# Longer weight runs, byte masks, later zero stores and separate column tiles in a diffusion backbone with recurrence and experts

## What is computed

```
sh1, sc1, g1, sh2, sc2, g2 = split(silu(cond) @ w_mod[l] + b_mod[l])
h  = rms_norm(x, norm1) * (1 + sc1) + sh1
... = split(h @ w_in[l])          # attention q, k, v; recurrence q, f, f', i, g; two gates
x += g1 * ((sig(ga) * (attn @ w_br_attn) + sig(gh) * (rec @ w_br_hgrn)) @ w_out[l])
h  = rms_norm(x, norm2) * (1 + sc2) + sh2
gates = top-1 group, then top-2 of its 4 experts, from sigmoid(h @ w_router)
x += g2 * sum_e gates[e] * (silu(h @ w_gate[e]) * (h @ w_up[e])) @ w_down[e]     # 16 experts, D_FF 512
```

## Time and profile before

| what | value |
|---|---|
| median of 3 runs | 1604.6 us (1602.77 to 1606.4) |
| the profiled execution's own time | 1598.92 us |
| its span | 1597.1 us |
| TensorE busy | 1401.8 us, 88% of the span |
| VectorE busy | 519.8 us |
| ScalarE busy | 335.0 us |
| GpSimd busy | 240.2 us |
| moved by DMA | 351.96 MB, mean 220 GB/s |

### The profile page before, as it was taken

The page is one execution under the profiler, slowest core; times in us unless marked ns, Lnnn a source line. Parts: engine busy times, 40 slices in busy tenths (PEclk is TensorE's granted clock), DMA queues, the critical chain, the costliest instruction groups (busy, mean ns, idle before and its releaser), DMA issues.

```text
span 1597.1 us, 18517 instructions
## 1 busy us (share of the span) xinstructions
PE 1401.8 (88%) x7179; PEld 768.5 (48%) x7180; DVE 519.8 (33%) x1041; ACT 335.0 (21%) x495; POOL 240.2 (15%) x213
## 2 busy tenths in 40 slices
PE   4699999899998899989965999988999598999882
PEld 1365545656554444544423655566654344444441
DVE  1333423744113411121125344278311521111114
ACT  1105533651101100100101065265100100001010
POOL 2260003841000000000012600186100000000001
PEclk9899999999999899999986999999999899999996
DMA  9635453176424999996984331211414444999994
GB/s 344 246 109 189 181 208 109 53 253 261 158 106 150 363 380 396 399 339 248 398 304 156 109 106 54 106 53 53 145 53 158 184 166 177 339 396 397 396 395 178
DMA packets 157043, 351.96 MB, mean 220 GB/s; under 512 B 5880, under 2 KB 13128, under 8 KB 156992
## 3 DMA queue, kind: packets, MB, share of 16 engines
q1 hardware_dynamic: 138208, 314.48, 53.0%
q0 software_dynamic: 6576, 22.80, 4.0%
q10 hardware_dynamic: 12208, 13.98, 2.6%
HBM read 335.69 MB, written 15.55 MB: 220 GB/s over the span
## 4 chain that ended last, share of the span: by engine, by line
PE 71%; DVE 10%; SPq 7%; DMA 6%; ACT 3%; issue 2%; POOL 0%; DVEq 0%; ACTq 0%; POOLq 0%
PE pG L1401 21%; PE pS L1481 10%; PE pG L1393 9%; SPq L472 6%; PE pG L1496 5%; PE pG L1623 5%; PE pG L1489 4%; DMA ring<-in_w_mod_dram 2%; PE pX L1322 2%; PE pX L1481 2%; DVE ring L1005 2%; PE pG L1355 2%; DMA ring<-in_w_exp_up_dram 1%; DVE modb L1007 1%; PE pX L1447 1%
## 5 line engine op out<-in xcount | busy, mean ns | idle before, releaser
L1401 PE MATMUL pG<-hT,ring 128*128 128x384 f32 x896 | 299.5, 488 | 1.6 <-ACT gen L842 1.6
L1481 PE MATMUL pS<-ring,gen 128*64 128x256 f32 x2048 | 229.8, 381 | 11.5 <-DMA ring<-in_w_exp_up_dram 9.5
L1401 PEld LDWEIGHTS pG<-hT,ring 128*128 128x128 f32 x896 | 168.0, 191 | 115.5 <-issue 4.7
L1481 PEld LDWEIGHTS pS<-ring,gen 128*64 128x64 f32 x2048 | 148.1, 138 | 100.5 <-issue 19.2
L1393 PE MATMUL pG<-ring,hT 128*128 128x512 f32 (+1 forms) x384 | 150.0, 548 | 1.4 <-DVE hT L964 0.7
L1496 PE MATMUL pG<-ring,gen 128*64 128x512 f32 x512 | 116.9, 598 | 5.2 <-DVE gen L1278 5.2
L1273 DVE TENSOR_TENSOR gen<-pS,gen 128x256 f32<-128x256 f32 x32 | 13.6, 425 | 313.4 <-PE pS L1481 313.4
L1393 PEld LDWEIGHTS pG<-ring,hT 128*128 128x128 f32 x384 | 72.6, 192 | 72.1 <-issue 67.7
L660 POOL DMA_INDIRECT gen<-y_scr,idx x12 | 11.8, 985 | 628.5 <-ACTq L892 625.5
L1489 PE MATMUL pG<-hrow,gen 128*64 128x512 f32 x408 | 95.4, 603 | 2.2 <-DVE gen L1173 1.5
L871 ACT COPY gen<-pG 128x512 f32<-128x512 f32 x32 | 18.8, 586 | 348.6 <-PE pG L1496 348.6
(11 more groups left out here) (276 smaller groups left out, 1655.8 us busy)
## 6 DMA issues: line engine op xcount, KB each, us to landing
ring<-in_w_exp_up_dram SPq DMA_DIRECT2D x32, 2048.0 KB, 20.4
ring<-in_w_exp_down_dram SPq DMA_DIRECT2D x32, 2048.0 KB, 19.2
ring<-in_w_exp_gate_dram SPq DMA_DIRECT2D x32, 2048.0 KB, 18.3
ring<-in_w_mod_dram SPq DMA_DIRECT2D x24, 2048.0 KB, 9.4
ring<-in_w_in_dram SPq DMA_DIRECT2D x20, 2048.0 KB, 8.4
modb<-mod_scr POOLq DMA_DIRECT2D x20, 512.0 KB, 9.2
y_scr<-gen ACTq DMA_DIRECT2D x72, 128.0 KB, 5.5
ring<-in_w_out_dram SPq DMA_DIRECT2D x4, 2048.0 KB, 10.1
```

Of the source, the lines that this page charges most:

```text
L1401: ins = pe.matmul(ps[:, 0:TOK], w[:, k, c0:c0 + P], src[:, k, :], start=(k == 0), stop=(k == nk - 1))
L1481: ins = pe.matmul(dst[64 * hf:64 * hf + 64, 0:256], x[:, k, :], w[:, k, 256 * hf:256 * (hf + 1)], start=(k == 0), stop=(k == KC - 1))
```

## The change

- Expert gate and up weights are loaded with rows 8p to 8p+7 in partition p, one run of 16 KB; down weights as two runs of 8 KB. The order of the 1024 features and of the 512 hidden values changes to match: the second norm writes `hrow` in permuted order, with a stride of 512 bytes from one element to the next, and the product of gate and up writes with the same stride between the two values of a pair. The router weights are loaded in the matching order, one run of 512 bytes in each partition.
- The masks come as bytes and straight into `masks`, without the int32 detour through `ring` and without the cast.
- The zero stores to `y_scr` move from the head of ACT's program to SP, behind the load of the `ff` weights.
- On POOL the norm weight now waits for the first `w_mod` piece and so does x, and the small tensors wait for the fourth.
- The four bias products of a `mod` go to four column tiles; the two sums of a pair go to column tiles 0 and 1.

```
-                    src = a[("w_exp_gate", "w_exp_up")[part]][L, e, :, :].rearrange("(k p) n -> p k n", p=P)
-                    dst = ring[:, s0 + part, :].rearrange("p (k n) -> p k n", k=KC)
+                    src = a[("w_exp_gate", "w_exp_up")[part]][L, e, :, :].rearrange("(p k) n -> p (k n)", p=P)
+                    dst = ring[:, s0 + part, :]
                 else:
-                    src = a["w_exp_down"][L, e, :, :].rearrange("(k p) n -> p k n", p=P)
-                    dst = ring[:, s0 + part, :].rearrange("p (k n) -> p k n", k=4)
+                    src = a["w_exp_down"][L, e, :, :].rearrange("(a p c) n -> p a (c n)", a=2, p=P)
+                    dst = ring[:, s0 + part, :].rearrange("p (a m) -> p a m", a=2)
...
                     unit(L, name)
+                    if (L, name) == (0, ("ff", 0)):
+                        sp.wait_ge(zeroed, 1)
+                        for i, r in enumerate(range(NE * BLK, YROWS, P)):
+                            sp.dma_start(y_scr[r:r + P, :].rearrange("p (a c) -> p a c", a=4),
+                                         bc(zeros, [P, 4, 256], 1)).then_inc((*e_ydma, v_dma)[i % 3], 16)
...
+            pool.wait_ge(landed[0], 16)
             load_norm(0, 0)
-            pool.wait_ge(landed[1], 16)
             pool.dma_start(xs[:, 0, :], a["x_prompt"][0]).then_inc(x_in, 16)
             pool.dma_start(xs[:, 1:3, :], a["x_sample"][0].rearrange("(t p) c -> p t c", p=P)).then_inc(x_in, 16)
+            pool.wait_ge(landed[3], 16)
...
-            pool.dma_start(wr[:, :, :], a["w_router"].rearrange("(k p) e -> p k e", p=P)).then_inc(small_in, 16)
+            pool.dma_start(wr[:, :, :], a["w_router"].rearrange("(p k) e -> p k e", p=P)).then_inc(small_in, 16)
...
-            pool.dma_start(masks32, a["masks"]).then_inc(small_in, 16)
+            pool.dma_start(masks[:, :, :].rearrange("p s t -> p (s t)"), a["masks"]).then_inc(small_in, 16)
...
-                act.copy(mod_parts(m)[0:32, :], ps[0:32, :]).then_inc(ms_evac, 1)
+                r = 32 * (m % 2)
+                act.copy(mod_parts(m)[r:r + 32, :], ps[r:r + 32, :]).then_inc(ms_evac, 1)
...
-                    link(dve.scalar_tensor_tensor(hrow[:, t, :], xs[:, t, :], stat[:, t:t + 1], modb[:, 1, cnd, :],
-                                                  ALU.mult, ALU.mult))
-                    dve.tensor_tensor(hrow[:, t, :], hrow[:, t, :], modb[:, 0, cnd, :], ALU.add).then_inc(h_ready, 1)
+                    if which == 0:
+                        h, x, scale, shift = hrow[:, t, :], xs[:, t, :], modb[:, 1, cnd, :], modb[:, 0, cnd, :]
+                    else:
+                        h = hrow[:, t, :].rearrange("p (k c) -> p c k", k=KC)
+                        x, scale, shift = (v.rearrange("p (c k) -> p c k", k=KC)
+                                           for v in (xs[:, t, :], modb[:, 1, cnd, :], modb[:, 0, cnd, :]))
+                    link(dve.scalar_tensor_tensor(h, x, stat[:, t:t + 1], scale, ALU.mult, ALU.mult))
+                    dve.tensor_tensor(h, h, shift, ALU.add).then_inc(h_ready, 1)
...
-                    dve.tensor_copy(masks[:, :, :].rearrange("p s t -> p (s t)"), masks32).then_inc(masks_ready, 1)
-                    dve.wait_ge(masks_ready, 1)
...
-                        dve.tensor_tensor(actb, bank[3][:, 0:256], gsil, ALU.mult).then_inc(e_act, 1)
+                        dve.tensor_tensor(by_pairs(actb), pairs(bank[3][:, 0:256]), pairs(gsil),
+                                          ALU.mult).then_inc(e_act, 1)
...
-                                  w[:, 2 * q + k, :], start=(k == 0), stop=(k == 1 and q > 0))
-                for j in range(4):
-                    r = 4 * (m % MODS) + j
-                    ins = pe.matmul(ps[0:32, P * j:P * (j + 1)], ident[:, r:r + 1].broadcast_to([P, 32]),
-                                    brow[:, m // MODS, :], start=False, stop=(j == 3))
+                                  w[:, 2 * q + k, :], start=(k == 0), stop=False)
+                for q in range(4):
+                    r = 4 * (m % MODS) + q
+                    ins = pe.matmul(ps[32 * q:32 * q + 32, P * q:P * (q + 1)], ident[:, r:r + 1].broadcast_to([P, 32]),
+                                    brow[:, m // MODS, :], start=False, stop=True)
...
-                finish_group(pe.matmul(ps[0:32, :], const[:, C_SEL:C_SEL + 32], mod_parts(m),
+                r = 32 * (m % 2)
+                finish_group(pe.matmul(ps[r:r + 32, :], const[:, C_SEL:C_SEL + 32], mod_parts(m),
                                        start=True, stop=True))
```

More of the change, by code:

```diff
@@ L142, in shape_constants @@
         c[:, C_SIN + HD * t:C_SIN + HD * (t + 1)] = np.sin(ang[t * P:(t + 1) * P]) * sign
-    masks = np.zeros((P, LEV_STEPS, P), np.int32)
+    masks = np.zeros((P, LEV_STEPS, P), np.uint8)
     s, t = np.arange(P)[:, None], np.arange(P)[None, :]
@@ L259, in build @@
         zeros = S[:, 7936:8192]
-        masks32 = S[:, 0:LEV_STEPS * P].bitcast(I32)
         pG = [ctx.enter_context(nc.psum_tensor(f"pG{i}", [P, 512], F32)) for i in range(2)]
@@ L273, in build @@
         cst_ready = sem("cst_ready")
-        masks_ready = sem("masks_ready")
         lb_ready = sem("lb_ready")
@@ L674, in _ @@
             act.sem_inc(e_y, 1)
-            act.wait_ge(zeroed, 1)
-            for i, r in enumerate(range(NE * BLK, YROWS, P)):
-                act.dma_start(y_scr[r:r + P, :].rearrange("p (a c) -> p a c", a=4),
-                              bc(zeros, [P, 4, 256], 1)).then_inc((*e_ydma, v_dma)[i % 3], 16)
             act.wait_ge(setup_in, 16 * 5)
@@ L703, in mod_store @@
                     dst = mod_scr[m // MODS, cnd:cnd + 1, 512 * (m % MODS):512 * (m % MODS + 1)]
-                    act.dma_start(dst, mod_parts(m)[16 * cnd:16 * cnd + 1, :]).then_inc(mod_stored[m % 2], 16)
+                    act.dma_start(dst, mod_parts(m)[r + 16 * cnd:r + 16 * cnd + 1, :]).then_inc(mod_stored[m % 2], 16)
             def mods_behind(L, kind):
@@ L1181, in xT_src, with pairs, by_pairs @@
                     return bank[b].rearrange("p (c a s) -> p c a s", c=4, a=2)
+                def pairs(x):
+                    return x.rearrange("p (q c) -> p q c", c=2)
+                def by_pairs(x):
+                    return x.rearrange("p (c q) -> p q c", c=2)
                 def aT_dst(dst):
@@ L1296, in _ @@
                                 dve.wait_ge(v_act, b + 1)
-                                dve.tensor_tensor(act_o, bank[7][:, 0:256], gsil_o, ALU.mult).then_inc(v_dve, 1)
+                                dve.tensor_tensor(by_pairs(act_o), pairs(bank[7][:, 0:256]), pairs(gsil_o),
+                                                  ALU.mult).then_inc(v_dve, 1)
                                 dve.wait_ge(v_pe, b * 5 + 7)
```

## The result

The changed kernel takes **1580.8 us** (median; 1578.8 to 1582.4) where the kernel before, run beside it, takes 1605.5 (1602.8 to 1606.6). The ratio is 0.9848, with an interval of 0.9831 to 0.9866: 24.7 us faster. The forecast was 1573 with a range of 1564 to 1590, so the number is inside the range. It lies just above the 1568 to 1580 that the forecast called its own, and nearer to the price of rival 1 (1587) than to 1573.

The account below looks back on a forecast made before the run. TensorE was taken to bound the kernel (71% of the wait chain), with DMA at the start and in layer 1's last experts. 13.5 + 5.1 + 1.2 + 0.6 + 11.1 = 31.5 us off 1604.6 gave 1573, range 1564 to 1590.

Parts of the forecast that it names:

- rival 1: Second norm and overflow blocks: the stride costs a second cycle per element, 1.07 us for each of 12 instructions; 1587, chance 27%.
- Start, 13.5 and 0.6 for piece 3: Kernel start: clearing loads ahead of the fourth modulation piece saves 13.5 us; spreading piece 3's bias saves 0.6.
- Column tiles, 5.1: Modulation pieces 4 to 11: bias spread over four column tiles saves 0.64 us per piece, 5.1 us in all.
- Experts of layer 1, 11.1: Last experts of layer 1: long weight runs load fast enough that TensorE never waits, 11.1 us off.
- the experts loaded ahead: Expert weights, layer 1: two experts loaded ahead are worth 12.6 us of slack before the first wait.
- The fitted price per packet (10 ns): DMA queues: 10 ns per packet and 0.0386 ns per byte, giving 15.3 us per expert, or 428 GB/s.
- Rivals 2 and 4: Expert loads: (2) long runs no faster, period 16.55, 1584, chance 9%; (4) 16 KB runs slower than 2 KB, 1625, 4%.
- rival 3: Kernel start: it shortens little, small tensors land late or the fourth piece keeps its time; 1587, chance 9%.
- It pays nothing for the stride, and I take 0.: Second norm, both layers: writes and reads with 512 bytes between elements cost 0, judged from a 12-element memset.
- the rivals' bound of 1 us: Strided product of gate and up in four overflow blocks, not covered by TensorE's gather: 0 to 1 us.

Follow-up runs that it names:

- ScalarE's version: Changed kernel with contiguous second norm and natural router weights; ScalarE writes a reordered copy of the rows behind the router for the gathers: 1569.5 us, ratio 0.9773.
- before, again: The kernel before, unchanged, in a second profiled execution: 1607.6 us.
- start alone: Kernel before with only the first stage's loads and masks changed; column tiles, expert loads and second norm as before: 1589.7 us, ratio 0.9896.
- start and tiles: Kernel before with the changed start and the column tiles for bias and sums; expert loads and norm as before: 1580.8 us, ratio 0.9840.
- long runs, no stride: Kernel before with changed start, column tiles and long expert weight runs, without strided writes; output not the reference's, one block less: 1550.5 us, ratio 0.9665.
- strided reads: Changed kernel with second norm and gate times up writing contiguously and reading in steps (32 B, 8 B) instead: 1582.3 us, ratio 0.9847.
- strided, zero stores first: Changed kernel with the zero stores of y_scr (3.1 MB) back at the head of ScalarE's queue: 1586.6 us in one execution.
- strided, small tensors early: Changed kernel with small tensors and masks no longer held until the fourth modulation piece has landed: 1579.6 us in one execution.
- copy strided: Changed kernel with the reordering moved from the second norm to the copy of the gathered rows, weights in 8 KB runs: 1581.4 us, ratio 0.9853.
- the same, operation done twice: Kernel with the reordering in the copy of gathered rows, plus the second norm's first operation done twice, contiguous: 1592.8 us, ratio 0.9926.
- six patterns: Changed kernel with the second norm in six access patterns, one per tile; output not the reference's, total not compared.
- TensorE's stride: Changed kernel with contiguous second norm; TensorE's router transposes and gathers read the rows in steps of 32 B: 1678.2 us in one execution.

## Why the prediction was right, and where it failed

- **Start, 13.5 and 0.6 for piece 3.** Right, if rather low: 14 to 16 us in the traces against the first profile (2.6 more against the second), 16.9 in the medians. The fourth piece came at 32.7 (forecast 33), the first projection at 51.3 (52). The small tensors were issued from 32.7 us, and VectorE waited for nothing at 50. How the 13.5 divides is less sure: the working had some 10 for the zero stores, and put back alone they cost 6.7; with the 1 to 3 of the small tensors that leaves 5 us or more that no run takes apart. TensorE's first projections ran longer in after, 33.4 us for 31.2 by the chain, with a granted clock of 0.75 in their first 9 us. That is not the change's: six of the eleven executions with the new start took 31.0, and the second one of the kernel before took 33.1.
- **Column tiles, 5.1.** Right: a pair of pieces with its sums takes 5.8 us for 7.1 (107.82 to 113.64, and 120.95 to 128.04 before), 0.64 a piece as worked out, and the stretch with the eight pieces was 5.5 us shorter.
- **Experts of layer 1, 11.1.** Right in mechanism: 426 GB/s for a forecast 428, TensorE never waits, all periods 14.75. The trace of after has 12.4 us against one profile of before and 10.9 against the other, ScalarE's version 10.8 to 11.2. The queue still takes longer for an expert than TensorE (6.55 MB at 426 GB/s are 15.4 us); the experts loaded ahead cover it, as worked out. The fitted price per packet (10 ns) held. By the rule in the Trainium skill (DMA: Bandwidth & Descriptors, "Why small descriptors are slow (HBM only)") the estimate was 413 GB/s; the measurement decides, and a packet costs more than that rule says. Rivals 2 and 4 are out, and rival 3 by the start.
- **"It pays nothing for the stride, and I take 0."** This step failed. Four memsets of 12 elements were taken as the measure of 1024 elements, and they don't show it: at the norm's 0.66 ns for each element they would have taken 8 ns more than they did. Whether they are too short or a memset is another case isn't shown. Twelve instructions pay 0.68 us, 8.2 in all. Rival 1 had the mechanism right but a price of 1.07, more than half as much again. The overflow blocks pay as the rivals' bound of 1 us said: the strided product takes 0.60 us for 0.43 in each of four, 0.7 in all.
- **What the sum left out even so.** From the change to ScalarE's version it is 12 us by the ratios, uncertain by some 5, where 8.2 are VectorE's own. The traces say more. Behind the norm stands a router whose products run at the clock that TensorE was left with. Its sixteen products and the first expert's sixty-four in layer 1, in the kernel before and then in after:

```profile
1261.27 5.32 PE L1631 MATMUL pS<-hT,wr 128*16 128x384 f32 x16 [0.77 <-DVE hT L964]
...
1285.25 8.81 PE L1481 MATMUL pS<-ring,gen 128*64 128x256 f32 x64 [0.97 <-DVE gen L1266]
```
```profile
1254.77 8.16 PE L1644 MATMUL pS<-hT,wr 128*16 128x384 f32 x16 [0.77 <-ACT hT L735]
...
1281.23 7.13 PE L1494 MATMUL pS<-ring,gen 128*64 128x256 f32 x64 [0.97 <-DVE gen L1276]
```

Before has the router at a granted clock of 1.00 and pays in the first expert (0.81); after has it the other way round (0.65, then 1.00). So the stretch must be measured to the second expert's gate and up products:

| norm to second expert, us | layer 0 | layer 1 | both | median |
|---|---|---|---|---|
| before | 54.9 | 49.8 | 104.7 | 1605.5 |
| before, again | 56.6 | 50.7 | 107.3 | |
| start alone | 58.6 | 49.9 | 108.6 | 1589.7 |
| start and tiles | 55.8 | 49.3 | 105.1 | 1580.8 |
| long runs, no stride | 55.9 | 49.9 | 105.7 | 1550.5 |
| ScalarE turns | 56.0 | 50.9 | 106.9 | 1569.5 |
| after (strided) | 61.7 | 55.6 | 117.3 | 1580.8 |
| strided reads | 62.1 | 55.7 | 117.8 | 1582.3 |
| strided, zero stores first | 61.6 | 55.7 | 117.3 | 1586.6, one run |
| strided, small tensors early | 59.9 | 55.9 | 115.8 | 1579.6, one run |
| copy strided | 56.5 | 51.5 | 107.9 | 1581.4 |
| the same, operation done twice | 61.8 | 56.1 | 117.8 | 1592.8 |

The six with an adjacent norm and copy have a mean of 106.4, the four with a strided norm 117.1: 10.7 us apart, and the two groups don't overlap. 8.2 of it are VectorE's own; the other 2.5 are TensorE's products at the lower clock, and they lie within what executions of one layout differ by (2 to 4 us). The doubled operation gives 9.9 for 7.7 of its own. (The runs with six patterns and with TensorE's stride do other work there and are left out.) In the same stretch, up to the first expert of layer 1, after and ScalarE's version differ little in the clock (third number from the end):

```profile
1240.43:1281.23 40.80, 23.50 (x77) 12.40 (x78) 25.75 (x66) 3.25 (x5) 1.05 (x2) 0.63 0.33 136
```
```profile
1233.16:1269.21 36.05, 22.85 (x77) 12.31 (x78) 21.64 (x66) 8.59 (x8) 1.05 (x2) 0.65 0.37 155
```

Of the 4.75 us between them 4.1 are VectorE's and 0.65 TensorE's. So the stride's own price explains most of the loss, and a part for the clock on top of it is likely but not shown.

In sum: 31.5 forecast, 24.7 measured. Start, tiles and long runs together gave 36 us (ScalarE's version), some 5 more than the sum had, and the strided norm with what follows from it took 11 to 12 that stood in the sum at nothing. So it is in part luck that the number came within 8 us: two errors of opposite sign. And it is the rivals, above all the one with the stride, that stretched the range as far as 1580.8.

## What to carry to other kernels

- A layout that pleases the DMA queue must be paid for by some engine. Ask which engine does the reordering and who waits for it: measured against the version where an engine that idles behind the router does it, the same permutation cost 11 to 12 us in the norm, as much in a copy that TensorE waits for in each period, and 109 in TensorE's own reads (one execution).
- A price per element is not read from a row of 12 elements. If the trace has no row of the size in question, don't put the lower bound into the sum as if it were measured.
- The granted clock moves a loss from one stage into the next. Compare stretches that begin and end at the same work, over several executions, and not the same microseconds of two kernels.
- A kernel whose output feeds a router does other work when its numbers change: count the blocks before comparing two times.

## What the runs showed of the hardware

- VectorE on fp32: adjacent elements or steps of 8 bytes 1.28 us for 1024 elements, written in steps of 16 to 512 bytes 1.94 to 2.07, read in steps of 32 bytes 2.09; the operation that reads and writes in steps of 512 pays once (1.91 for 1.22). In a copy from PSUM it was 0.65 ns for each of 512 elements (1026 for 692 ns).
- ScalarE's copies of 1024 elements with strided writes took 1.82 us; it has no contiguous copy of that size in these traces, and 512 elements took 0.58.
- TensorE's moving operand with steps of 32 bytes: 5.67 us for 2.75. Its transposes of 128 columns in the same steps: unchanged (mean 376 ns in both).
- Weight loads with all packets at 2 or 4 KB moved 396 GB/s, at 8 KB 422 or 423, at 16 and 8 KB 426 or 427.
